# Expert tokens dealt over groups of eight partitions instead of filling an expert's quarters from the first lane up

## The reference

```python
def moe(h, w_router, b_router, we_g, we_u, we_d, ws_g, ws_u, ws_d):
    s = jax.nn.sigmoid(jnp.dot(h, w_router))
    # the best 4 of 8 groups of experts, in them the best 8 experts: eidx, with weights wts
    ...
    def step(acc, blk):                       # a block: up to 128 tokens of one expert
        e, tok, wt = blk
        xb = h[tok]                                              # gather
        hb = jax.nn.silu(xb @ we_g[e]) * (xb @ we_u[e])          # gate and up, 1024 x 256 each
        return acc.at[tok].add(wt[:, None] * (hb @ we_d[e])), None   # down, 256 x 1024
    ...
    shared = (jax.nn.silu(h @ ws_g) * (h @ ws_u)) @ ws_d
    return routed + shared
```

## Time and profile before

| | before |
|---|---|
| three timed executions, median (us) | 1124.86 (1123.6 to 1125.34) |
| the profiled execution, its own time (us) | 1125.71 |
| its span, first to last instruction (us) | 1123.9 |
| TensorE (PE) busy | 1092.7 us, 97% of the span |
| PE in the expert stage, 535 to 1015 us | 480.00 of 480.00 us |
| DMA engines in the same stretch | mean busy share 1.00, 412 GB/s |
| VectorE (DVE) busy | 463.5 us, 41% |
| GpSimd (POOL) busy | 135.3 us, 12% |

### The profile page before, as it was taken

One profiled execution on the slowest core, in us unless ns is written; L12 is line 12 of the kernel. 1 busy time (PEld: TensorE's weight loads), 2 busy tenths in 40 slices (PEclk: granted clock), 3 DMA queues, 4 the chain that ended last, 5 costly groups with the idle time before them and its releaser, 6 DMA issues.

```text
span 1123.9 us, 16923 instructions
## 1 busy us (share of the span) xinstructions
PE 1092.7 (97%) x6443; PEld 574.4 (51%) x6443; DVE 463.5 (41%) x1286; ACT 236.7 (21%) x516; POOL 135.3 (12%) x163
## 2 busy tenths in 40 slices
PE   6999999999999999999999999999999999999986
PEld 3456677777877544754343443443444444343332
DVE  2218541565456645843275233233233232231157
ACT  4131241223133223211111111111111111111111
POOL 0210000000020010121111112112111111111100
PEclk9999999999999999999999999999999999999999
DMA  9857622021170286789999999999999999999698
GB/s 371 325 201 302 227 79 75 1 85 34 80 255 18 91 286 229 273 302 403 418 425 424 423 417 426 422 415 398 424 411 379 422 408 392 415 395 370 222 415 341
DMA packets 51654, 337.16 MB, mean 300 GB/s; under 512 B 9636, under 2 KB 14088, under 8 KB 30830
## 3 DMA queue, kind: packets, MB, share of 16 engines
q1 hardware_dynamic: 33710, 287.32, 63.4%
q0 software_dynamic: 17856, 48.68, 11.7%
HBM read 311.30 MB, written 37.24 MB: 310 GB/s over the span
## 4 chain that ended last, share of the span: by engine, by line
PE 91%; DMA 4%; DVE 2%; ACT 1%; issue 1%; SPq 0%; DVEq 0%; POOLq 0%; ACTq 0%
PE bank L1565 30%; PE bank L1588 15%; PE bank L1261 10%; PE bank L1280 5%; PE bank L1553 4%; DMA mem<-expert_out_rows 3%; PE bank L1379 3%; PE bank L1174 3%; PE bank L1380 3%; PE bank L1497 3%; PE bank L1258 3%; PE bank L1149 1%; PE bank L1576 1%; PE bank L1344 1%; PE bank L1158 1%; PE bank L1132 1%
## 5 line engine op out<-in xcount | busy, mean ns | idle before, releaser
L1565 PE MATMUL bank<-mem 128*32 128x512 f32 (+2 forms) x1504 | 318.8, 594 | 0.6 <-DVE mem L2251 0.6
L1565 PEld LDWEIGHTS bank<-mem 128*32 128x32 f32 (+2 forms) x1504 | 106.7, 127 | 194.2 <-issue 194.2
L1588 PE MATMUL bank<-mem 128*32 128x512 f32 (+2 forms) x752 | 164.2, 596 | 1.1 <-ACT mem L1069 1.1
L2251 DVE COPY mem<-bank 128x512 f32<-128x512 f32 x48 | 33.2, 692 | 283.3 <-PE bank L1553 283.3
L1261 PE MATMUL bank<-hT,mem 128*128 128x288 f32 x512 | 133.3, 409 | 1.0 <-ACT mem L939 1.0
L1261 PEld LDWEIGHTS bank<-hT,mem 128*128 128x128 f32 x512 | 93.8, 190 | 25.8 <-issue 2.4
L1565 PE MATMUL bank<-x_sb,mem 128*32 128x512 f32 (+2 forms) x400 | 105.8, 593 | 0.0
L1588 PEld LDWEIGHTS bank<-mem 128*32 128x32 f32 (+2 forms) x752 | 51.7, 127 | 72.0 <-issue 71.1
L1069 ACT ACTIVATE mem<-bank 128x256 f32<-128x256 f32 x48 | 18.4, 384 | 313.0 <-PE bank L1576 312.8
L2266 DVE COPY hT<-bank 128x512 f32<-128x512 f32 x48 | 33.2, 692 | 85.4 <-PE bank L1588 85.4
L794 POOL DMA_INDIRECT mem<-ffn_in_rows,idxg x32 | 32.9, 1028 | 264.7 <-DVE idxs L2247 211.0
(11 more groups left out here) (400 smaller groups left out, 1279.3 us busy)
## 6 DMA issues: line engine op xcount, KB each, us to landing
mem<-k_w_exp SPq DMA_DIRECT2D x52, 2048.0 KB, 19.3
mem<-in_w_exp_down SPq DMA_DIRECT2D x52, 1024.0 KB, 20.6
x_sb<-k_w_exp SPq DMA_DIRECT2D x12, 2048.0 KB, 23.8
mem<-k_w_ada SPq DMA_DIRECT2D x8, 2048.0 KB, 9.3
mem<-k_w_in SPq DMA_DIRECT2D x7, 2048.0 KB, 9.4
hT<-in_w_exp_down SPq DMA_DIRECT2D x12, 1024.0 KB, 22.2
mem<-expert_out_rows SPq DMA_DIRECT2D x6, 2048.0 KB, 16.5
mem<-k_w_head SPq DMA_DIRECT2D x4, 2048.0 KB, 18.4
```

The lines of the kernel that those rows point to most:

```text
L1565: i = mm(bank[sl, :], xT[:, j % 2, c * BLK + sl.start:c * BLK + sl.stop], wview(r)[0][:, c, :], start=c == 0, stop=c == KC - 1)
L1588: i = mm(ps[4 + hf][sl, :], hhT[:, k * BLK + sl.start:k * BLK + sl.stop], wview(r)[1][:, k, hf * 512:(hf + 1) * 512], start=k == 0, stop=k ...
```

## The change

The row of numbers that positions are compared with is no longer `iota` but a permutation of it, kept as bf16 in a new tensor `deal`, one for segments of 1, 2, 3 and 4 quarters each. For a segment of k quarters (32k lanes), position p = 4k·r + e goes to lane 8e + r, with e from 0 to 4k-1 and r from 0 to 7. The first 4k tokens go to the first lane of each group of eight partitions, the next 4k to the second lane, and so on. Which tokens share a segment, the number of instructions in the loop over blocks and every shape in it stay as they are.

```diff
+DR = 8
...
+        deal = sb("deal", [P, 10 * QS], BF16)
...
+        def dealt(k):
+
+            return deal[:, k * (k - 1) // 2 * QS:k * (k + 1) // 2 * QS]
...
             dve.memset(oneb, 1.0)
+            for k in range(1, P // QS + 1):
+                cp(dealt(k).rearrange("p (e r) -> p e r", r=DR), iota[:, 0:k * QS].rearrange("p (r e) -> p e r", r=DR))
             cp(trib, cst["tri"][:, :])
...
                 w = pm.shape[-1]
-                return stt(pm, p.to_broadcast([P, NT, w]), off, iota[:, 0:w].unsqueeze(1).to_broadcast([P, NT, w]),
+                return stt(pm, p.to_broadcast([P, NT, w]), off, dealt(w // QS).unsqueeze(1).to_broadcast([P, NT, w]),
                            ALU.add, ALU.is_equal)
```

## The result

The changed kernel takes 1135.1 us, the median of four runs (1133.27 to 1135.78), beside 1124.49 us for the kernel before (four runs, 1123.6 to 1125.34): 1.0092 times as long, interval [1.0074, 1.0109], some 10 us. The forecast was 1125.2 us with a range up to 1127.6. The rival "eight crowded engines hold up the weights" (1128 us, chance 0.14) is what happened, only larger.

A forecast was written before the change was run, and what follows sets the result against it. PE was taken to bound the kernel; casts 0, comparison 0, first gathers 0, last scatter +0.3 and weights 0 us, added to the median 1124.86 us, gave 1125.2 us, with a range of 1123.3 to 1127.6 us.

The forecast's parts named there:

- eight crowded engines hold up the weights: Expert stage, rival: half the engines serve weights late, PE waits 2 to 4 us, 1128 us in all; chance 0.14.
- the bound and the covers: Expert stage: PE busy 480.00 of 480.00 us bounds it; the casts and comparison are hidden, cost 0.
- The casts: Before the router's result: four casts take 0.7 us, hidden by the memset and VectorE's 1.56 us idle; cost 0.
- The comparison: On VectorE, 640 columns with one input now bf16: same 822 ns expected, cost 0.
- PE's idle time ahead of block 1: At the start, before block 1: 0.35 + 0.62 us, expected to stay within 0.5 us of 0.97.
- the lanes: Indirect DMAs: each engine has four neighbouring lanes in each of two quarters, so the change moves the crowd without thinning it.
- The last scatter: Block 47, on the path: fullest engine goes from 6 to 8 rows, +0.3 us.
- the term for the weights: Expert stage: later weight loads stay within their margin, taken as 0, up to +2 us for the range.
- 7 x 2 x 0.17 = 2.4 us: Blocks 30 to 46: extra work on the fullest engine, 134 rows against 127, each moved twice.
- My comparison of 369 with 375: All 48 blocks: fullest engine's rows before and after, of 4608; an even deal would be 288.
- only if no queue runs empty in between: Weight loads: condition under which the 2.4 us of extra work barely stays within the margin of 2.5 and 3.2 us.
- a late load delays only once: Expert stage, argument against the held-up weights: a late load also delays the release of the next.

The follow-up runs named there:

- e2: The changed kernel with tokens dealt over groups of four lanes instead of eight: 1124.21 us, 0.9993 of the kernel before.
- e3: The changed kernel with lanes inside each group of eight filled in the order 0, 4, 1, 5, 2, 6, 3, 7: 1125.44 us, 1.0003 of the kernel before.
- e9: The change's fill in partitions 0 to 63 only, partitions 64 to 127 evened out: 1129.81 us, 1.0042 of the kernel before.
- e10: The change's fill in partitions 64 to 127 only, partitions 0 to 63 evened out: 1132.46 us, 1.0071 of the kernel before.
- e7: The change's deal in blocks 26 to 47 only, earlier blocks filled as in the kernel before: 1125.85 us, 1.0008 of the kernel before.
- e5: The changed kernel, but in partitions 64 to 127 lanes 4 to 7 of each eight fill first: 1134.83 us, 1.0074 of the kernel before.
- e4: The changed kernel, but lanes 4 to 7 of every eight fill first, crowding the other eight engines: 1131.66 us, 1.0056 of the kernel before.

## Why the prediction was wrong

**Right: the bound and the covers.** PE is the bound, and DMA time saved in the stage is worth next to nothing: e2 took some 8 us off the landings of the kernel before, for no gain that can be told from noise. The casts cost nothing, though by other numbers than mine. The changed kernel's timeline:

```profile
457.40 3.31 DVE L2097 CAST deal<-c_full 128x32 bf16<-128x32 f32 x4
...
460.64 0.21 DVE L2098 CAST mem<-c_full 128x128 bf16<-128x128 f32 x1
...
460.96 0.24 DVE L2100 TENSOR_SCALAR mem<-mem 128x320 bf16<-128x320 bf16 x1
```

I gave them 0.7 us, and they took 3.31 us beside GpSimd's memsets. But the operation that took 3.00 us in the earlier trace rows, and now stands behind the memset, takes 0.24. In both traces it is what VectorE does while GpSimd's memsets run (up to 460.83 before, 460.58 now) that takes 3 us; why is not shown. The router's result still comes later (a wait of 1.02 us is left of 1.56). The comparison takes 824 ns, against 822 in the earlier trace rows. PE's idle time ahead of block 1 is still 0.35 + 0.62 us.

**Right: the lanes.** That an engine has four neighbouring lanes in each of two quarters was read from one burst. That the shares are fours and not eights is now shown by e3, which repairs the loss by alternating the fours inside each eight. That e9 and e10 make four shares late and the change eight says that an engine's lanes lie in one half of the partitions; which two quarters it has no run shows. (Of the 77 small packets that the prediction calls empty lanes, block 47 explains only 128 - 67 = 61; the 67 full rows stand.) By the Trainium skill (page "DMA: Bandwidth & Descriptors", section "The descriptor swizzle") the change crowds every second engine; the trace agrees as far as it goes, with eight early and eight late shares in the row of the changed kernel above; which engines they are it doesn't say. The last scatter was forecast at +0.3 us and took +0.37.

**Wrong: the term for the weights**, taken as 0 and at most +2 us. It is 4.96 us of waits and 3.44 us of lower clock. It failed at three points.

*The late landing was priced by the fullest engine's extra rows*, "7 x 2 x 0.17 = 2.4 us". The loads around 934 and 945 us came 9.3 and 9.8 us later. One part is, as far as the runs tell, that the fullest engine is not the latest one. Before, the engines of the upper half of the partitions had at most 311 rows; the change gave four of them 373 to 375. e9 and e10 show what this does: the lower half's crowd ends at 18.8 us, 3.4 behind the kernel before, the upper half's at 23.2, with nearly equal counts. My comparison of 369 with 375 was blind to this, as it took all engines to be equally fast and asked only for the fullest. The other part is that I counted the rows of blocks 30 to 46 only. e7 shows that a crowd of the late blocks alone leaves the landing at 15.3 us. What was put on an engine before still counts, so the sum has to run over the whole stage, and for each engine: in e7 the fullest one has 373 rows over the stage, nearly as many as with the change (375), but the upper half's four have 276 to 358 in place of 373 to 375. The prediction named the condition ("only if no queue runs empty in between") and did not draw the sum from it, though the DMA share of 1.00 spoke for it.

*The margin was read where it was smallest before*, 2.5 us at the load of 755.0 and 3.2 us at that of 1029.3. PE waited first for the load issued at 934.2, which before had landed at 934.4 + 20.7 = 955.1 us for 961.83, 6.7 us ahead. The load at 755 now takes 28.3 in place of 25.5 us and lands at 783.1, in the last 0.1 us before its use. A lateness that differs from load to load has to be set against each load's own margin.

*The price of a wait was taken as its length.* Two of the three waits cost another 1.70 and 1.74 us of lower clock. That is 3.4 of 8.9 us, more than the whole width that I had given upward.

The chance of 0.14 for the held-up weights rested on these three points. That "a late load delays only once" held for the first wait, behind which none came for 74 us. Near the end the loads were late again, twice.

## What to carry to other kernels

When a change moves DMA rows between engines, compare the load on each engine before and after, over the whole stretch in which the DMA share is 1.00, and not the two maxima over a part of it. Set the later landings against the margin of each load by name. Price a wait of PE above its length: here 2.1 to 2.9 us of waiting on a PE otherwise always busy cost another 1.7 us in five of eight cases and nothing in three, and 4.4 us another 2.8. Look for it in the busy time of the matmuls behind it, where no list of waits shows it.

## What was not expected of the hardware

**Equal rows, unequal engines.** With 368 to 375 rows on each of four engines, the four late shares of one load land 14 to 19 us after issue when the lower half is crowded (e9) and 17 to 23 us when the upper half is (e10); the spread within a half is 4.6 and 6.5 us. The 4 or 5 rows that the upper ones have more from block 26 to 40 are worth some 1.5 us by the prediction's price, not the whole difference. The records don't say which engine a share belongs to, and what makes one slower stays open.

**The clock behind a wait.** Waits of 2.08, 2.16, 2.45, 2.54 and 2.87 us were followed by a granted clock of 0.79 to 0.81 over 8 to 9 us, for +1.7 us; one of 4.41 us in e5 by 0.71 over 9.9 us, where a group of 32 matmuls took 9.86 in place of 7.04 us. Three waits of 1.66, 1.86 and 1.89 us (e5, e10, e4) were not. But the length alone does not decide: the 2.71 us of e4 and two of e10 (2.58 and 2.09 us) left the clock at 1.00, as the windows of e10 over its wait of 2.58 us and the group behind it show:

```profile
1034.00:1036.60 2.60, 0.07 (x2) 0.00 (x0) 0.69 (x1) 0.60 (x1) 0.92 (x1) 1.00 0.99 402
1036.65:1043.70 7.05, 7.05 (x33) 2.64 (x33) 0.00 (x0) 0.00 (x0) 0.01 (x1) 1.00 0.94 375
```

Both kinds occur at the same expert (1040.17 in the changed kernel slow, 1040.05 in e4 not). What tells them apart was not found.
